# Attention's output projection in token rows, with the residual by transposes and the middle norm along the rows; another order of buffers for the weight loads

## The reference

```python
h = token_mixer(x, w_in, g_sb, g_dil, w_out, rel_bias)   # y = head norms of 16 heads of 64, then y @ w_out
x = layer_norm_2(ALPHA * x + h, ln1_g, ln1_b)            # the middle norm, ALPHA = 2 ** 0.25
h = grouped_moe(x, w_router, b_router, w_gate, w_up, w_down)   # softmax over 16 experts, top 2 of one group
x = layer_norm_2(ALPHA * x + h, ln2_g, ln2_b)
```

## Time and profile before

| what | us |
|---|---|
| median of 3 runs | 1584.67 |
| lowest and highest | 1584.25, 1585.34 |
| the profiled execution | 1583.29 |
| its span, first to last instruction | 1581.6 |
| PE busy | 1470.9 (93%) |
| PEld busy | 948.8 (60%) |
| DVE, ACT, POOL busy | 509.7, 328.2, 152.0 |
| mean granted TensorE clock | 0.983 |
| read from HBM | 401.79 MB, 255 GB/s over the span |

### The profile page before, as it was taken

One profiled execution on the slowest core, in us unless ns is written; L12 is line 12 of the kernel. 1 busy time (PEld: TensorE's weight loads), 2 busy tenths in 40 slices (PEclk: granted clock), 3 DMA queues, 4 the chain that ended last, 5 costly groups with the idle time before them and its releaser, 6 DMA issues.

```text
span 1581.6 us, 21236 instructions
## 1 busy us (share of the span) xinstructions
PE 1470.9 (93%) x8151; PEld 948.8 (60%) x8151; DVE 509.7 (32%) x1074; ACT 328.2 (21%) x722; POOL 152.0 (10%) x170
## 2 busy tenths in 40 slices
PE   6899999999999999999998789999999999569996
PEld 2577777787588888875554359977534443124432
DVE  2567777667630311144221120042511110101002
ACT  2343343433431200021010011161100000000001
POOL 1334433334200000000000000000000000000000
PEclk9999999999999999999999999999999999989999
DMA  9711111111655344547799998405499999999996
GB/s 383 319 54 40 53 40 40 40 40 53 264 214 195 140 153 168 172 160 318 315 423 423 423 421 337 145 16 208 186 424 421 424 402 424 423 424 424 422 421 265
DMA packets 58860, 403.98 MB, mean 255 GB/s; under 512 B 6833, under 2 KB 6961, under 8 KB 12448
## 3 DMA queue, kind: packets, MB, share of 16 engines
q1 hardware_dynamic: 52992, 382.96, 59.9%
q0 software_dynamic: 5792, 19.95, 4.2%
HBM read 401.79 MB, written 1.10 MB: 255 GB/s over the span
## 4 chain that ended last, share of the span: by engine, by line
PE 72%; SPq 11%; DMA 6%; DVE 5%; issue 2%; ACT 2%; POOL 1%; DVEq 0%; ACTq 0%; POOLq 0%
PE bank L695 71%; SPq L525 10%; DMA ring<-in_moe 2%; DMA o_heads<-in_moe 2%; DMA arena<-in_moe 2%; ACT arena L1464 1%; DVE arena L1907 1%; POOL arena L637 1%; PE bank L1159 1%; DMA xc<-in_xc 1%; DMA decay_rows<-arena 0%; SPq L536 0%; DVE arena L1896 0%; DVE arena L1898 0%; ACT hc L1464 0%
## 5 line engine op out<-in xcount | busy, mean ns | idle before, releaser
L695 PE MATMUL bank<-arena 128*128 128x128 f32 (+7 forms) x3112 | 520.0, 338 | 30.8 <-DVE arena L1898 15.1
L695 PEld LDWEIGHTS bank<-arena 128*128 128x128 f32 (+3 forms) x3112 | 380.5, 183 | 181.1 <-issue 95.0
L1464 ACT ACTIVATE arena<-bank 128x256 f32<-128x256 f32 (+2 forms) x373 | 161.2, 447 | 1065.3 <-PE bank L695 794.2
L695 PE MATMUL bank<-ring,arena 128*64 128x512 f32 (+2 forms) x1232 | 339.4, 625 | 39.0 <-DMA ring<-in_moe 17.9
L695 PEld LDWEIGHTS bank<-ring,arena 128*64 128x64 f32 (+2 forms) x1232 | 101.7, 135 | 196.4 <-issue 194.4
L695 PE MATMUL bank<-hc,head_w 128*128 128x512 f32 (+1 forms) x384 | 162.4, 525 | 0.5 <-DVE hc L1831 0.5
L2253 DVE TENSOR_TENSOR arena<-arena,bank 128x256 f32<-128x256 f32 x43 | 18.1, 421 | 332.5 <-ACT arena L1464 332.5
L695 PE MATMUL bank<-hc,arena 128*64 128x512 f32 (+1 forms) x216 | 93.9, 612 | 1.9 <-DMA ring<-in_moe 1.2
L695 PE MATMUL bank<-hc,ring 128*128 128x256 f32 x416 | 91.2, 379 | 0.0
L695 PEld LDWEIGHTS bank<-hc,ring 128*128 128x128 f32 x416 | 78.4, 190 | 11.1 <-issue 0.8
L1464 ACT ACTIVATE arena<-arena 128x512 f32<-128x512 f32 (+4 forms) x139 | 66.0, 507 | 39.9 <-DVE arena L1848 25.4
(11 more groups left out here) (269 smaller groups left out, 1301.5 us busy)
## 6 DMA issues: line engine op xcount, KB each, us to landing
ring<-in_moe SPq DMA_DIRECT2D x154, 1024.0 KB, 23.1
ring<-in_dense SPq DMA_DIRECT2D x59, 1024.0 KB, 9.5
arena<-in_moe SPq DMA_DIRECT2D x51, 1024.0 KB, 24.6
hc<-in_moe SPq DMA_DIRECT2D x27, 1024.0 KB, 22.6
head_w<-in_moe SPq DMA_DIRECT2D x14, 1024.0 KB, 24.4
xc<-in_moe SPq DMA_DIRECT2D x14, 1024.0 KB, 21.1
o_heads<-in_moe SPq DMA_DIRECT2D x14, 1024.0 KB, 20.6
first_w<-in_moe SPq DMA_DIRECT2D x14, 1024.0 KB, 22.5
```

The lines of the kernel that those rows point to most:

```text
L695: return nc.tensor.matmul(out, lhsT, rhs_, start=start, stop=stop, **kw)
L1464: return nc.scalar.activation(out, in_, func, **kw)
```

## The change

It has two parts. **The buffers:** a load takes the entry of `free` with the lowest count of uses, so the buffer that is spent first, in place of the first entry; and `squares` joins for the second mixture after the last norm of the first block, as the middle norm no longer writes it. **The projection and the norm:** each 128 tokens (qt) get a sum of 1024 channels in two PSUM banks (4 and 5, 6 and 7). `residual_rows` puts `X` there by 8 transposes per qt; `out2(p, qt)` adds a head pair's part by 4 matmuls with 512 moving columns, `w_out_2` being laid out by rows of head pairs. In place of ALPHA * `X` + h the sum is `X` + h / ALPHA: the head gains are divided by ALPHA once, and the 1e-5 by its square. Mean and variance come from DVE's row statistics, as in the last norm; ACT makes the root; DVE and ACT each write one half of the normalised rows, PE transposes them back (16), and ACT and DVE apply gain and bias while they copy them into `X`. The router matmuls go by qt. The three `keep_warm` matmuls of this stretch stand together behind the projection.

```diff
@@ -154,9 +155,9 @@
-             second + RING + 5: ("tokens", "out2_made", KT),
-             second + RING + 6: ("buffers", "out2_made", KT),
-             second + RING + 7: ("squares", "ln_var", 1),
+             second + RING + 5: ("tokens", "out2_made", 4),
+             second + RING + 6: ("buffers", "out2_made", 4),
+             second + RING + 7: ("squares", "norm_summed", 2),
...
-        home, used = free.pop(0)
+        home, used = free.pop(min(range(len(free)), key=lambda i: free[i][1]))
...
             pool.wait_ge(s["tables_landed"], 80 + 32)
-            pool.wait_ge(s["residual"], 2 * KT + 1)
+            pool.wait_ge(s["att_normed"], KT)
             pool.dma_start(arena[:, 10752:10752 + KT * (GROUPS1 + E1 + E2)], t["router_w"]).then_inc(s["router_landed"], 16)
...
-            def keep_warm(n):
+            def keep_warm(n, spare=7):
 
                 for _ in range(n):
-                    mm(bank[7][:, :].rearrange("p (a b) -> p a b", a=4), ones[:, :], times(M("ident"), 4))
+                    mm(bank[spare][:, :].rearrange("p (a b) -> p a b", a=4), ones[:, :], times(M("ident"), 4))
...
@@ -1077,20 +1079,29 @@
             def route(m, width, experts):
 
 
-                keep_warm(2)
+                if m == 0:
+                    keep_warm(2)
...
+                else:
                     for qt in range(QT):
-                        ins = mm(logits[qt], src[:, k, qt * P:(qt + 1) * P], router_w[m][:, k, :], False,
-                                 k == KT - 1 and qt == QT - 1, skip_group_check=True)
+                        for k in range(KT):
+                            if k < 4:
+                                pe.wait_ge(s["route_in"], KT + 4 * qt + k + 1)
+                            else:
+                                pe.wait_ge(s["route_scaled"], KT + 4 * qt + k - 3)
+                            ins = mm(logits[qt], src[:, k, qt * P:(qt + 1) * P], router_w[m][:, k, :], False,
+                                     k == KT - 1 and qt == QT - 1, skip_group_check=True)
                 ins.then_inc(s["logits_made"], 1)
...
-            def out2(j, ks_, first, last):
-                w = block_of(SECOND_G, O20 + j, N_SECOND - 1) if first else block_view(SECOND_G, O20 + j)
-                for k in ks_:
-                    if j == 0:
-                        pe.wait_ge(s["att_normed"], PAIRED.index(k) + 1)
-                    ins = mm(bank[4 + j % 4][:, 0:SEQ], w[:, k, :], o_att[:, k, :], k == PAIRED[0], k == PAIRED[-1])
-                    if last and k == ks_[0]:
-                        release(ins)
-                if last:
-                    ins.then_inc(s["out2_made"], 1)
-                    block_ends(O20 + j, N_SECOND - 1)
+            def residual_rows(qt):
+                for k in range(KT):
+                    ins = mm(bank[Z_ROWS[2 * qt + k // 4]][:, (k % 4) * P:(k % 4 + 1) * P], X[:, k, qt * P:(qt + 1) * P],
+                             M("ident"), k % 4 == 0, False, is_transpose=True, skip_group_check=True)
+                    release(ins)
+
+            def out2(p, qt):
+                what = SLOT["dense", SECOND_G + O20 // BLOCKS + p]
+                pe.wait_ge(landed[HOME[what]], LANDED_AT[what])
+                pe.wait_ge(s["att_normed"], 2 * p + 2)
+                for i in range(BLOCKS):
+                    w = group_view(SECOND_G + O20 // BLOCKS + p)[:, i * D:(i + 1) * D]
+                    for half in range(2):
+                        ins = mm(bank[Z_ROWS[2 * qt + half]][:, :], o_att[:, PAIRED[2 * p + i], qt * P:(qt + 1) * P],
+                                 w[:, half * 512:(half + 1) * 512], False, p == H2 // 2 - 1 and i == 1, skip_group_check=True)
+                        if p == H2 // 2 - 1 and i == 1:
+                            ins.then_inc(s["out2_made"], 1)
+                if qt == 1 and p < H2 // 2 - 1:
+                    ins.then_inc(slots_used, 1)
...
@@ -1413,45 +1432,31 @@
                 if p + 1 < pairs:
                     dl_scores(p + 1)
                 else:
-                    for j in range(2):
-                        out2(j, PAIRED[0:4], True, False)
+                    residual_rows(0)
+                    out2(0, 0)
                 dl_turn(p, 1)
                 if p + 2 < pairs:
                     sb_scores(p + 2)
                 if p + 1 == pairs:
-                    for j in range(2, 4):
-                        out2(j, PAIRED[0:4], True, False)
+                    residual_rows(1)
+                    out2(0, 1)
                 dl_values(p)
-            for j in range(2):
-                out2(j, PAIRED[4:6], False, False)
+            out2(1, 0)
             head_sum(pairs - 1)
-            for j in range(2, 4):
-                out2(j, PAIRED[4:6], False, False)
-
-            def mean_sum(i, k):
-
-                pe.wait_ge(s["residual"], KT * (i + 2) + k + 1)
...
-            def variance_sum(i):
-
-                keep_warm(1)
-                for k in range(KT):
-                    pe.wait_ge(s["ln_sq"], KT // 2 * i + k // 2 + 1)
-                    ins = mm(bank[VAR_BANKS[i]][:, 0:SEQ], ones[:, :], HS[:, k, :], k == 0, k == KT - 1)
-                ins.then_inc(s["ln_var"], 1)
-
-            for j in range(KT):
-                if j >= 4:
-                    pe.wait_ge(s["residual"], 2 * KT + j - 3)
-                out2(j, PAIRED if j >= 4 else PAIRED[6:], j >= 4, True)
-                if j > 0:
-                    mean_sum(0, j - 1)
-            mean_sum(0, KT - 1)
-            variance_sum(0)
+            out2(1, 1)
+            for qt in range(QT):
+                out2(2, qt)
+            for qt in range(QT):
+                out2(3, qt)
+            mm(bank[3][:, 0:P], ones[:, :], M("ident")).then_inc(slots_used, 1)
+            keep_warm(3, 3)
+            for qt in range(QT):
+                for half in range(2):
+                    pe.wait_ge(s["ln_rows_by_act" if half else "ln_rows_by_dve"], qt + 1)
+                    for k in range(4 * half, 4 * half + 4):
+                        at = (k % 4) * P
+                        ins = nc.tensor.transpose(bank[2 * qt + half][:, at:at + P], ln_rows1[:, qt, k * P:(k + 1) * P], M("ident"))
+                    ins.then_inc(s["ln_turned"], 1)
             route(1, E2, E2)
             mixture(1)
...
             def route(m, experts):
-                shift(m)
+                if m == 0:
+                    shift()
...
-            def layer_norm(i):
-                act.wait_ge(s["ln_mean"], i + 1)
-                act_fn(norm_m, bank[MEAN_BANKS[i]][:, 0:SEQ], ACT.Copy, scale=1.0 / D).then_inc(s["ln_mean_copied"], 1)
-                for p in range(KT // 2):
-                    act.wait_ge(s["ln_centred"], KT // 2 * i + p + 1)
-                    act_fn(HS[:, 2 * p:2 * p + 2, :], X[:, 2 * p:2 * p + 2, :], ACT.Square).then_inc(s["ln_sq"], 1)
-                act.wait_ge(s["ln_var"], i + 1)
-                rsqrt(norm_r, bank[VAR_BANKS[i]][:, 0:SEQ], 1.0 / D, LN_EPS).then_inc(s["rnorm"], 1)
-
-            layer_norm(0)
+            def root(nth, qt, eps_of):
+                act.wait_ge(s["v_stats"], nth + qt + 1)
+                rsqrt(bn_r[:, qt:qt + 1], bn_mv[:, qt, 1:2], 1.0, eps_of).then_inc(s["rnorm"], 1)
+
+            for qt in range(QT):
+                root(1, qt, LN1_EPS)
+                act.wait_ge(s["ln_shift"], qt + 1)
+                act_fn(ln_rows1[:, qt, 512:D], bank[Z_ROWS[2 * qt + 1]][:, :], ACT.Identity, scale=bn_r[:, qt:qt + 1],
+                       bias=bn_mv[:, qt, 0:1]).then_inc(s["ln_rows_by_act"], 1)
+            for qt in range(QT):
+                act.wait_ge(s["ln_turned"], 2 * qt + 1)
+                for k in range(4):
+                    act_fn(X[:, k, qt * P:(qt + 1) * P], bank[2 * qt][:, k * P:(k + 1) * P], ACT.Identity, scale=V("ln1_g")[:, k:k + 1],
+                           bias=V("ln1_b")[:, k:k + 1]).then_inc(s["route_in"], 1)
             route(1, E2)
...
                         ALU.mult, ALU.mult).then_inc(s["att_normed"], 1)
 
             dve.wait_ge(s["x3_ready"], KT)
+            link(ts_(V("g_heads"), V("g_heads"), 1.0 / ALPHA, None, ALU.mult))
             sb_sum(0)
             dl_shift(0)
             dl_scale(0)
...
-            for j in range(KT):
-                dve.wait_ge(s["out2_made"], j + 1)
-                stt(X[:, j, :], X[:, j, :], ALPHA, bank[4 + j % 4][:, 0:SEQ], ALU.mult, ALU.add).then_inc(s["residual"], 1)
-
-            def layer_norm(i, name):
-                dve.wait_ge(s["ln_mean_copied"], i + 1)
-                for p in range(KT // 2):
-                    tt_(X[:, 2 * p:2 * p + 2, :], X[:, 2 * p:2 * p + 2, :], times(norm_m, 2), ALU.subtract).then_inc(s["ln_centred"], 1)
-                dve.wait_ge(s["ln_centred"], KT // 2 * (i + 1))
-                dve.wait_ge(s["rnorm"], 4 + i + 1)
-                for k in range(KT):
-                    stt(X[:, k, :], X[:, k, :], V(name + "_g")[:, k:k + 1], norm_r, ALU.mult, ALU.mult
```

(25 more changed lines are left out.)

46 lines of the change are left out of this document (20 added, 26 removed).

## The result

The changed kernel takes **1570.69 us** (median of 4 runs, 1569.22 to 1570.85); the kernel before, beside it, 1585.01 (4 runs, 1584.25 to 1589.15). The ratio is 0.9902, 95% interval 0.9884 to 0.9920: 14.3 us faster. The prediction was 1568.3, with a range from 1564 to 1578. The profiled execution of the changed kernel took 1570.85, with a span of 1569.1 against 1581.6 before: 12.5 us less, where the sum had 16.4. That is the difference to be explained, 3.9 us of span.

What follows compares the result with a forecast made beforehand. The second mixture was taken as a string of loads whose end follows its start, set by PE. -9.3 - 1.8 - 5.3 = -16.4 us, from 1584.7 to 1568.3 us; range 1564 to 1578.

Steps and rivals of the forecast that it cites:

- both parts as summed: Buffers, projection and middle norm all pay as costed, -16.4 us in sum; chance 0.60, own range 1565.5 to 1571.5.
- the hole was not hidden: Rival on the first mixture's 9.3 us without transfers: closing it is hidden, only -7.1, 1577.6; chance 0.12.
- the norm's new chain did not replace the old one: Rival in the middle norm: DVE and ACT take 7 us longer, projection and norm worth nothing, 1575.4; chance 0.06.
- the second mixture kept its clock at its start: Rival: PE loses its clock early in the second mixture, slower, 1588.3 with 40 us at half rate; chance 0.04.
- The bound: Second mixture is a string of loads: 435.3 us from restart to last landing, its end following its start.
- Part 1: Buffer rule in the first mixture: loads 93 to 102 go out earlier, closing a 9.3 us hole; -9.3, bounds 6.2 and 10.5.
- Part 2a: Projection up to its end, T: 16 new transposes cost 1.75 us, mean sums and waiting go; -1.8 us.
- Part 2b: From the projection's end, T, to DVE reading the logits: 8.9 us instead of 14.2; -5.3 us.
- rival 1: Clock falls at T + 2.7 (T: projection's end), slowing transposes and narrow matmuls: +5.3, 1573.6; chance 0.14.
- The statistics beside PE: Middle norm: qt 1's row statistics, done at T + 2.4 (T: projection's end), are covered by PE, 1.2 us to spare.
- The rule on transposes: Transposes don't count as work raising the clock, so the stretch behind the projection would run at the lower level, as rival 1.

Runs made afterwards that it cites:

- the buffer rule alone: The kernel before with only the new allocation line (the buffer that is spent first); old projection and middle norm: 1577.15 us, ratio 0.9951.
- one more `keep_warm`: The changed kernel with one more wide matmul between the 16 transposes back and the router's matmuls: 1570.48 us, ratio 0.9901.
- warm last wait: The changed kernel with four unread wide matmuls ahead of the `down` matmuls of the first mixture's last quad: 1566.28 us, again 1566.94.
- in order of use: The kernel before, old buffer rule, with the first mixture's loads sent in the order in which they are spent: 1581.86 us, ratio 0.9976.
- the kernel without `keep_warm`: The changed kernel without the three `keep_warm` matmuls behind the projection: 1569.3 us, ratio 0.9897.
- three `keep_warm`, and two: The warm last wait with its three `keep_warm` behind the projection (1566.28 us, again 1566.94), and the same kernel with two there (1565.90 us).
- the interleaved kernel: The warm last wait with qt 0 finished first, its transposes and router matmuls covering qt 1's statistics: 1567.24 us, again 1565.53.

## Why the prediction was right, and where it was short

The forecast case (both parts as summed) is what happened, 2.4 us above its point and inside its own range of 1565.5 to 1571.5. The upper end of that range stood for a first part of 6.2 us or a clock that falls late, and the second is what came; for the lower ends, 1565.5 and 1564, the prediction gives no full working, as its best bound for part 1 (10.5 in place of 9.3) takes only 1.2 us off. The rivals fell: the hole was not hidden (ten profiles with the new rule have 199.0 to 199.3 where the two with the old one and the old order have 208.2 and 208.3), the norm's new chain did not replace the old one, and the second mixture kept its clock at its start. Step by step:

1. **The bound.** "Whatever brings the first `up` matmuls of the second mixture forward brings the end forward by the same amount." Right: the restart moved by 12.85 us and the span by 12.5, and from the restart to the last landing all thirteen profiles have 434.7 to 435.9.
2. **Part 1, -9.3.** The hole was worth 9.27 at the last quad, and PE could follow. (435.3 us over 173 loads are 2.52 each, not 2.49; for the four loads in the hole that is 0.1 us.) The step that failed is the next one: "All that follows, the attention loads, DVE's and POOL's work, hangs on the first mixture's end and moves with it." It forgot that the last wait itself grows when the loads come another way. PE waited 3.86 us instead of 3.44, the clock went down behind it, and the last quad and what follows took 1.70 us more. All six profiles without warm matmuls whose last wait was 3.86 or more have 31.9 to 33.2 in this stage; the two with 3.44 and 3.45 have 30.3. That idle PE is the cause is shown by the warm wait; that the half microsecond more of it is what decides is not, as a wait of 3.46 from 899.2 in the kernel before was followed by a low clock, and so were waits of 3.17 and 3.21 near 893 in two other profiles (the buffer rule alone, one more `keep_warm`):

```profile
904.00:906.00 2.00, 2.00 (x12) 0.54 (x8) 0.00 (x0) 0.00 (x0) 0.00 (x0) 0.50 1.01 426
```

Its place among what PE did before may count as much as its length. The prediction looked for a falling clock in the middle norm and in the second mixture, but not at the wait that its own first part moves. Another 0.8 us went to a later start of the mixture. That is scatter and not the change: with the changed kernel's code up to there, the start lay between 713.2 and 715.8. (The last 0.4 lies behind the restart, inside its scatter of 434.7 to 435.9.)
3. **Part 2a, -1.8.** Measured -1.71, with 8 transposes in 0.87 (1.75 for 16, as priced).
4. **Part 2b, -5.3.** The pieces were right, since with the clock up the logits come at T + 9.03 against the 8.9 forecast (the warm last wait). The mis-sized term is the 32 narrow matmuls, 4.5 us instead of 3.6: rival 1 in a smaller form. Why the clock falls there, without a wait of PE since 1054.4, no run shows. The clock fell at T + 7.8, not at T + 2.7 as that rival had it, so only the last part of them was slow. The yardstick had the same flaw: the old chain of 14.20 was one with a low clock at its end; two profiles of it with the clock up until the logits (the buffer rule alone, in order of use) have 13.37 (it fell 0.2 us before the logits in the first and behind them in the second). By its form alone part 2b is worth 13.37 - 9.03 = 4.3 us.
5. **The statistics beside PE.** The rows of qt 1 were ready at T + 2.8 (2.4 forecast), the last copy at T + 6.5 (7.0 forecast), and PE waited for neither. "Without them it would be the bound": in the kernel without `keep_warm` it was, by a wait of 1.61 us, though the dearer loss was the clock, which had no part in the sum as a price of leaving them out.

**The rule on transposes.** The trace first: with the warm last wait, the stretch of 16 transposes back and 32 narrow matmuls ran at 1.00 until the logits in two profiles (three `keep_warm`, and two), and in the changed kernel the clock fell only 5 us after the first of these transposes. The Trainium skill (TensorE: Matmul & The Clock Gate, Part 4: PE-mode transpose) says that transposes don't count as work that brings up the clock. Behind T a clock that was up stayed up through all 16. The first routing, with its own 16 transposes, also shows one that came up. In the second profile of the interleaved kernel it was at the lower level from 696.8, PE did nothing but these transposes from 696.93 on, and from 700.2 it had 1.00 again:

```profile
696.93 3.52 PE L1113 MATMUL bank<-first_w,hc 128*128 128x128 f32 x16
700.29 1.88 PE L697 MATMUL bank<-first_w,ones 128*128 128x512 f32 x4
```

```profile
697.00:700.00 3.00, 3.00 (x16) 3.00 (x16) 2.11 (x13) 0.21 (x1) 0.00 (x0) 0.50 1.01 429
700.20:701.00 0.80, 0.80 (x4) 0.47 (x3) 0.68 (x4) 0.00 (x0) 0.00 (x0) 1.00 1.01 430
```

It came up within the transposes in the profile with one more `keep_warm` too (at 700.6, transposes from 698.12 to 701.09); in the changed kernel's first profile it came up only at 702.9, 2.2 us into the wide matmuls behind them. So here the rule doesn't hold each time. Nor did the clock stay up when a wide matmul, the kind of work that the rule would count, stood between the transposes and the narrow matmuls behind T (5.29 us for the narrow ones). With keep_warm behind T the clock fell at T + 7.1 to T + 7.9 in four profiles and at T + 8.5 to T + 9.7 in the three with a warm last wait; why, is open.

## What to carry to other kernels

Cut the path at marks that both kernels have, and compare stage by stage: thirteen profiles then agreed to 0.1 or 0.3 us in most stages, and 3.5 of the missing 3.9 us had three addresses, one of them chance. Where a change makes loads come earlier, look at the waits that remain, the last one above all: where PE idles, the clock behind the wait may be lost, and four matmuls that nobody reads (3.7 us of idle time) bought back 1.7 us here. Filling buffers in the order of their last use gave 8.4 us here and sending the loads in the order of use 3.7, as the second sent two loads less ahead of a stop of the queue.

## What was not expected of the hardware

- The granted clock can hang on little: with 3.44 and 3.45 us of PE idle ahead of the last quad's `down` matmuls it stayed up in both profiles, with 3.86 us and more it fell in all six, while 3.17 to 3.46 us elsewhere was followed by a fall too. Length alone doesn't tell.
- A PE that waits for nothing can lose its clock: in the changed kernel, T + 7.8 is 7.8 us of matmuls and transposes without a wait, the last of them 16 columns wide. The profile calls PE busy there, but a half-matmul of 16 columns takes as long (3.59 us for 32 with the clock up, 0.112 each) as a transpose of 128 columns (1.84 for 16, 0.115), and weight loads fill 2.81 of the 3.00 us from 1092; whether that has to do with the fall was not tried. A 0.86 us wide matmul ahead of the narrow ones did not prevent it; a different order of the same work (interleaved) did in one profile, and kept the fall behind the logits (T + 7.5) in the other.
